# Queries and the first gate block of an attention layer computed by Strassen's seven products ahead of the head loop

## What is computed

```
proj = h @ w_in            # h: 520 tokens x 2048, w_in: 2048 x (4 * 2048 + 48)
q = proj[:, 0:2048]                          # 16 heads x 128
z = proj[:, 2048:8192]                       # three gate blocks: one per branch
gates = sigmoid(proj[:, 8192:8240])          # 3 branches x 16 heads
...
o_cmp = softmax(q @ k_compressed.T * SCALE + bias) @ v_compressed    # 31 keys
o_slc = attention over selected blocks        # the prompt has 8 blocks, all are selected
o_win = attention over a causal window of 512
y = sum over the branches of gates * o * silu(z)
return y @ w_out
```

## Time and profile before

| what | us |
|---|---|
| median of the runs | 2485.82 (2484.53 to 2487.34) |
| span of the profiled execution | 2482.8 |
| the profiled execution's own time | not listed apart; the median of the runs is 3.0 above its span |
| PE busy | 2421.4 (98% of the span) |
| DVE busy | 942.5 (38%) |
| ACT busy | 766.5 (31%) |
| POOL busy | 374.1 (15%) |
| matmuls of L2065 (dense and others of its helper) | 3 x 4896 |

### The profile page before, as it was taken

One profiled execution on the slowest core, in us unless ns is written; L12 is line 12 of the kernel. 1 busy time (PEld: TensorE's weight loads), 2 busy tenths in 40 slices (PEclk: granted clock), 3 DMA queues, 4 the chain that ended last, 5 costly groups with the idle time before them and its releaser, 6 DMA issues.

```text
span 2482.8 us, 49402 instructions
## 1 busy us (share of the span) xinstructions
PE 2421.4 (98%) x20902; PEld 2283.3 (92%) x20902; DVE 942.5 (38%) x1760; ACT 766.5 (31%) x1302; POOL 374.1 (15%) x505
## 2 busy tenths in 40 slices
PE   7999999999999999999999999999999999997997
PEld 6888888888899999999999999999999999966997
DVE  1236111221263353333534444444434443454333
ACT  1125111111232241111534334343434343432222
POOL 2002000790000000010402111111111111223000
PEclk9999999999999999999999999999999999999999
DMA  9985887576553446663633222323232323398232
GB/s 341 337 300 189 262 277 230 186 227 228 170 182 120 128 162 202 196 196 111 157 82 85 77 86 77 86 71 92 69 94 69 94 65 97 122 318 306 86 93 87
DMA packets 323392, 394.52 MB, mean 159 GB/s; under 512 B 20966, under 2 KB 287462, under 8 KB 320802
## 3 DMA queue, kind: packets, MB, share of 16 engines
q1 hardware_dynamic: 307554, 328.72, 42.1%
q0 software_dynamic: 15648, 62.97, 7.7%
HBM read 371.01 MB, written 42.69 MB: 167 GB/s over the span
## 4 chain that ended last, share of the span: by engine, by line
PE 91%; DVE 3%; ACT 2%; issue 1%; DMA 1%; SPq 1%; POOL 0%; ACTq 0%; DVEq 0%; POOLq 0%
PE acc L2065 70%; PE work L1980 4%; PE work L1920 2%; PE work L2215 2%; PE out_acc L2246 2%; PE work L2232 1%; PE work L2277 1%; PE acc L1920 1%; PE work L1968 1%; PE acc L2290 1%; PE out_acc L2241 1%; PE work L2206 1%; PE work L2151 1%; ACT probs L1189 0%; SPq L695 0%
## 5 line engine op out<-in xcount | busy, mean ns | idle before, releaser
L2065 PE MATMUL acc<-h_hi,w_hi 128*128 128x260 f32 x4896 | 1009.3, 287 | 7.1 <-issue 4.2
L2065 PE MATMUL acc<-h_hi,w_lo 128*128 128x260 f32 x4896 | 986.3, 283 | 0.0
L2065 PE MATMUL acc<-h_lo,w_hi 128*128 128x260 f32 x4896 | 984.5, 283 | 0.0
L2065 PEld LDWEIGHTS acc<-h_hi,w_hi 128*128 128x128 f32 x4896 | 753.4, 189 | 39.5 <-issue 37.3
L2065 PEld LDWEIGHTS acc<-h_hi,w_lo 128*128 128x128 f32 x4896 | 754.8, 189 | 0.0
L2065 PEld LDWEIGHTS acc<-h_lo,w_hi 128*128 128x128 f32 x4896 | 753.9, 188 | 0.0
L1298 DVE TENSOR_TENSOR w_lo<-raw,w_hi 128x1024 fp32r<-128x1024 f32 (+1 forms) x316 | 404.2, 1280 | 920.1 <-ACT w_hi L955 916.8
L955 ACT ACTIVATE w_hi<-raw 128x1024 fp32r<-128x1024 f32 (+1 forms) x316 | 332.9, 1054 | 1087.7 <-PE acc L2065 1077.8
L902 POOL TENSOR_TENSOR probs<-probs,row_stats 128x128 f32<-128x128 f32 (+3 forms) x128 | 110.2, 892 | 442.8 <-DVE row_stats L1675 442.8
L1980 PE MATMUL work<-rows_T_early,w_c_early 128*128 128x124 f32 x960 | 113.9, 278 | 1.6 <-DMA w_c_early<-in_w_ck 1.6
L1980 PEld LDWEIGHTS work<-rows_T_early,w_c_early 128*128 128x128 f32 x960 | 111.5, 195 | 1.9 <-issue 1.9
(11 more groups left out here) (355 smaller groups left out, 2016.9 us busy)
## 6 DMA issues: line engine op xcount, KB each, us to landing
ada<-in_w_ada SPq DMA_DIRECT2D x192, 512.0 KB, 4.9
raw<-in_w_in_b SPq DMA_DIRECT2D x128, 512.0 KB, 3.9
raw<-in_w_in_a SPq DMA_DIRECT2D x64, 512.0 KB, 5.0
raw<-in_w_kv SPq DMA_DIRECT2D x48, 512.0 KB, 3.6
raw<-in_w_out_a SPq DMA_DIRECT2D x32, 512.0 KB, 3.7
raw<-in_w_out_b SPq DMA_DIRECT2D x32, 512.0 KB, 3.6
pages_early<-in_cache_k_cmp SPq DMA_DIRECT2D x32, 256.0 KB, 4.1
pages_early<-in_cache_v_cmp SPq DMA_DIRECT2D x32, 256.0 KB, 5.0
```

Source lines behind the costliest of these rows:

```text
L2065: last = mm_(out[half][0:n, 0:HT], part[slot][:, kk, cols_], src[:, k, half * HT:(half + 1) * HT], start=(first and part is HI and src is ...
```

## The change

The projections of queries (16 heads) and of the first gate block are taken out of the head loop and made ahead of it, in 16 **pairs**: query columns of two heads and gate columns of the same two heads in turn. A pair is a 2x2 block product of a 2048 x 256 piece of weights, in blocks of 1024 x 128 (A11, A21, A12, A22: the first index is the output tile, the second the k half), with the tokens, in blocks of 1024 x 260 (b11, b12, b21, b22: k half, token half). Strassen's scheme in Winograd's form makes it of seven products of 8 k tiles x 3 = 24 matmuls, where the blocks one by one are eight. They run in the order P1, P5, P6, P4, P7, P2, P3, each into one bank (`block_product`, L2565), some started on top of an earlier one.

- Sums of weights (S1 to S4) are four DVE operations of 128x1024 a pair (L1890, L1896, L1900, L1906). Each product's weights are split by ACT (`block_hi`, L1354) and DVE (`block_lo`, L1871) into one of three buffers.
- Sums of tokens (T1 to T4) are made once: T1 by DVE in the normalising loop after tile 11, the other three by POOL after it (8 tiles x 260 columns each). ACT and DVE split them (`t_hi` L1344, `t_lo` L1880). `apply(1)` now keeps the normalised tokens in X rather than in three small buffers.
- The results are added by one ACT copy of P1, of P5 and of the last block, and five short DVE operations (`block_out`), scaled or passed through silu by ACT (`pair_out`, L1364, L1367), and stored to DRAM by SP (`pair_store`). The eight sample columns stay in SBUF.
- The gate quad now goes to `acc2` and `acc3`; its transposes (`gates_turn`) stand behind P1 of the first pair.
- The head loop has two quads (8 quarters) a turn, for gate blocks two and three (matmuls L2414, high parts L1113, low parts L1534). Queries and bias come back by SP (`head_tables`), the first gate block by POOL (`z_load`). The order of a turn is written anew: in unit u, PE turns the probabilities of unit n - 2, does half a quarter, the scores of unit n, another half, the values of n - 2, and the rest of the half quarters up to the next unit. Probabilities have two buffers. Where ACT and DVE split a quarter's weights is given by two tables (`MID`: between turning and exp; `LATE`: at a unit's end).

```diff
+Q_U, Q_Z, Q_MIX, Q_OA, Q_KV, Q_G, Q_P, Q_H, Q_OB = 0, 8, 16, 18, 26, 38, 39, 67, 83
+MID = {0: (1,), 3: (5,)}
+LATE = {0: (2,), 1: (3,), 2: (4,), 3: (6,), 4: (7,), 5: (8,)}
+FIRST_HALF = (0, 3, 5, 8, 11, 13, 16)
...
+            t1, t3 = X[:, 0:8, 0:HT], X[:, 0:8, HT:T]
+            nc.gpsimd.tensor_tensor(t3, b22, t3, ALU.subtract).then_inc(t_sums, 1)
+            nc.gpsimd.tensor_tensor(b22, b22, t1, ALU.subtract).then_inc(t_sums, 1)
+            nc.gpsimd.tensor_tensor(b21, b22, b21, ALU.subtract).then_inc(t_sums, 1)
...
+            hi(Q_G, 2)
+            t_hi(0)
+            hi(Q_G, 3)
+            block_hi(0)
+            block_hi(1)
+            t_hi(1)
             act.wait_ge(w_used, 4 * (Q_G + 1))
             for half in range(2):
+                last = nc.scalar.activation(GF[:, half * HT:(half + 1) * HT], D[2 + half][0:48, 0:HT], ACT.Sigmoid)
+            block_hi(2)
+            t_hi(2)
...
+                elif u in (2, 5):
+                    z_out(i, u // 3, 0)
+                    quarters(LATE[u])
+                    z_out(i, u // 3, 1)
...
+                for u in range(6):
+                    if not first or u >= 2:
+                        turned(i, u)
+                    quarters((u + 1,) if last_turn else MID.get(u, ()))
+                    softmax(i, u)
+                    if not first or u >= 2:
+                        weighed(i, u)
+                    factor(i, u)
+                    if not last_turn:
+                        quarters(LATE[u])
...
+                if s == S_P1:
+                    wait(pe, st_copied, 3 * q)
+                elif s == S_P5:
+                    wait(pe, st_added, 5 * q)
...
+                out = D[(0, 1, 3, 2, 3, 0, 1)[s]]
+                begin = s in (S_P1, S_P5, S_P6, S_P4)
+                for kk in range(8):
+                    for part, w, b in ((0, HB, b_hi), (1, HB, b_lo), (2, LB, b_hi)):
+                        last = mm_(out[:, 0:HT], w[slot_of(p)][:, kk, :], b[:, k0 + kk, at:at + HT],
+                                   start=(begin and kk == 0 and part == 0), stop=(kk == 7 and part == 2), skip_group_check=True)
...
+                for u in range(len(steps) - 1):
+                    n = 6 * i + u
+                    if n >= 2:
+                        turn(n - 2)
+                    half(steps[u])
+                    if u < 6:
+                        scores(n)
+                    half(steps[u] + 1)
+                    if n >= 2:
+                        values(n - 2)
+                    for h in range(steps[u] + 2, steps[u + 1]):
+                        half(h)
```

705 lines of the change are left out of this document (501 added, 204 removed).

## The result

The change takes 2493.69 us (median of 8 runs, 2491.74 to 2494.32), the kernel before 2485.79 in the 8 runs beside it. The ratio is 1.003, with a 95% interval of 1.002 to 1.004: 7.9 us **slower**. The forecast was 9.2 us faster.

What follows compares the result with a forecast made beforehand. The prediction took PE's instruction count to bound the kernel. It summed -46.0 + 6 + 13.4 + 19.9 - 3.5 (old idle) + 1 (loop entry) = -9.2 us, for a median of 2476.6 us, range 2458 to 2500.

Steps and rivals of the forecast that it cites:

- Matmuls, -46.0: Query and first gate blocks: 384 fewer matmuls at the dense 0.1197 us each, -46.0 us.
- The head loop, +19.9: Head loop: weight splits queued in order on ACT and DVE make PE wait, +19.9 us (10 to 45).
- 1.75 a turn at quarter 4: Head loop, unit 2 to 3: PE waits for quarter 4's low part, 1.75 us in 7 turns, +12.3.
- 1.1 at unit 2: Head loop, unit 1 to 2: PE waits for a split behind quarter 3's low part, 1.1 us, 6 turns, +6.6.
- The pairs, +6: Product stage, between pairs: P5 waits for the previous pair's last addition, 0.4 us, 15 times, +6 (0 to 12).
- The start, +13.4: Product stage's start: POOL's sums stop DVE and the sigmoid comes late; 14.6 less 1.2 earlier waiting, +13.4 us (6 to 18).
- The 0.6 at P1 and the 1.8 at P4: First pair: P1 waits 0.6 us for DVE, P4 1.8 us for the third token low part.
- the other end, 6: Start of the product stage: DVE loses only 1 us at each meeting with POOL, so the start costs 6 us.
- the rival of sharing: Start of the product stage: POOL and DVE share rather than lock, start costs 6, 2469 us; chance 0.08.
- I cost the DMA at nothing: Product stage: blocks in 512-byte pieces land in time, the tightest, A21, having 6.5 us; cost nothing.
- the first one: Head loop: in-order queues decide, a unit's round 0.5 us longer adds 21 us, 2498 us, slower; chance 0.27.
- Nearly all hidden: Head loop: splits come in time, the loop costs 6 instead of 20, 2463 or 2456 us; chance 0.15.

Runs made afterwards that it cites:

- e7: The change with ACT splitting the quarter's weights before the silu of the gate block's first half in units 2 and 5: 2480.84 us.
- e9: The change with the edits of e7 and e8 together: 2473.04 us.
- e6: The change with DVE adding a pair's last product before the third sum of weights instead of behind it: 2485.82 us.
- e2: The change with each of POOL's three token sums cut into 8 instructions of 260 columns: 2490.62 us.
- e5: The change with the twelve 4-byte gate stores made one store, reordered by twelve small loads after the head loop: 2491.34 us.
- e3: The change with PE's five gaps of the start filled with 97 matmuls that nobody reads: 2495.56 us.
- e1: The change with POOL's three token sums made by DVE between the low parts of the gate quarters: 2486.49 us.
- e8: The change with quarter 3's weights split in unit 2 behind the turned probabilities, not at the end of unit 1: 2493.40 us.
- e4: The change with the gates' transposes and DVE's copy of them behind P4 of the first pair instead of behind P1: 2495.74 us.
- e12: The change with e1, e4, e5 (its small loads spread over the samples' scores), e6, e7 and e8 together: 2449.98 us.

## Why the prediction was wrong

It put PE's waits of the head loop at their right places, and its time for that loop holds; the sign was lost in the product stage. The 18.5 us between the forecast of the span (-9.2) and the measured one (+9.3) are, row by row in the one profiled execution: 0.7 ahead of the gate quad, 1.9 to the end of the first pair, 4.2 of waiting for a block and 1.6 at half clock behind it, 3.7 for the handovers between pairs, 1.8 for the entry to the loop and steps a little over 0.1197, 1.6 in the head loop and 2.9 behind it. The numbers are rounded; the 2.9 lie within what the same instructions vary by.

- **Matmuls, -46.0**: this holds. Steps inside a product are 0.12, and the pair without its wait is 20.18, against 20.1 by 0.1197.
- **The head loop, +19.9**: mechanism and size hold. Forecast were 1.75 a turn at quarter 4 and 1.1 at unit 2 (counted in 6 turns, it came in 7); measured are 1.8 and 1.2, and taking them away is worth 12.9 (e7) and 7.8 (e9), 20.7 in all. The turn is 75.06.
- **The pairs, +6**: right mechanism, wrong size. The wait was 0.44, as forecast, but the restart behind it (a fourth part of a us) was not in the 6: a pair loses 0.68 against e6, 14 times, and 9.7 us up to the loop. It is worth 7.9 in the time.
- **The start, +13.4**: the rows came much as worked out (gate quarter 0 at 1223.38 for 1224.95, the third POOL sum over at 1232.87 for a wait "to 1235.9", the sigmoid done at 1246.6 for 1245.7, PE's wait at P7 1.9 for 1.7). The 0.6 at P1 and the 1.8 at P4 did not come. PE waited 8.5 us in all (1.52, 0.44, 1.92, 2.75 and 1.91), and four stretches at half clock took some 1.5 each; so it is in part luck that the forecast's 14.6 of pure waiting comes out. In e2 and the change POOL does hold DVE to the end of an instruction, so the other end, 6, and the rival of sharing are excluded. The sigmoid, too, stood behind a DMA: ACT came to it behind a block whose sum DVE began at 1240.53 after 3.13 us of waiting for a load.
- **The step that failed** is "I cost the DMA at nothing". Its slack of 6.5 us was reckoned from the landing of `v_group`, 3.3, in a stretch where nothing else disturbed it. Here twelve stores of 4-byte elements came just ahead of three blocks without a lead: 11.6 us to land, 4.2 waited (6.2 to 7.1 in e7 to e9), and a half-clock P1 behind the gap. The copy of this P1 came 8.4 us behind the 1270.3 that the forecast gives (1233.65 + 8 x 2.87 + 13.4 + 0.25), and without the stores (e5) it comes 6.2 earlier. The kernel before had the same stores, and loads of 12.2 us beside them, under dense work whose weights had a lead (PE's only wait in the loop's first 5 us is the 0.45 of the earlier trace rows); so the price stood in the trace that was read, and the earlier trace rows gave only a median. The list of what would make the forecast wrong had "PE waiting for a DMA" and "the granted clock ... falling in the start's gaps", but neither had a term in the sum or in the range of the start (6 to 18). Over the start the clock was 0.83, but of its 1.5 us stretches only the one in the second pair's P1 surely counts: what the others gave back in e3 was waited out in front of that P1. The DMA alone doesn't turn the sign: 5.8 of the 18.5 us are its wait and the stretch behind it. The mis-sized handover (3.7) is the second step.
- **The rivals**: the first one's time was near (2498 for 2493.7), by luck: its mechanism was not at work, as turns of 75.06 show no unit's round longer than counted. "Nearly all hidden" is what e9's loop shows for a changed order, not for this one.

## What to carry to other kernels

When a stage loses its lead (work that was spread over a loop is packed in front of it), look at every small transfer and table load that used to be free beside it, and give a term to each: a 4-byte store is no cost until something urgent is loaded beside it. The price may already stand in the trace of before, in the stretch where it was hidden: look at the landings there and not at the median of the page. Where two engines split weights in order, place each split by the row that waits for it, one by one: here the exchange of two lines was worth 12.9 us, and five such edits (e1, e5 to e8) turned a loss of 7.9 us into a gain of 36.9. A saved wait counts only if the next wait, or the clock behind the next gap, doesn't take it back; so test an edit that "did nothing" again once the wait behind it is gone (e8 in e9), and believe it when it still does nothing (e4 in e12).
